# Finishing one token tile early at five seams of a two-block transformer kernel, and a query slot computed with tokens as rows

## The reference

```python
m = hybrid_mixer(h, ...)      # compressed, selected and window attention + short convolution, @ w_o
h = layer_norm(ALPHA * h + m, ln1_g[l], ln1_b[l])
f = swiglu(h, ...) if l % 2 == 0 else moe_swiglu(h, ...)
h = layer_norm(ALPHA * h + f, ln2_g[l], ln2_b[l])
```

## Time and profile before

| | |
|---|---|
| median of 3 runs | 1381.17 us |
| lowest, highest | 1379.94, 1381.62 us |
| the profiled execution, span from first to last instruction | 1380.5 us, mean granted clock 0.995 |
| TensorE matmul, share of the span | 98% |
| VectorE, ScalarE, GpSimd | 71%, 56%, 8% |
| loaded and stored | 306.33 MB, mean 222 GB/s |

### The profile page before, as it was taken

How to read it: one execution, slowest core, us unless ns; L and a number is a source line. 1 busy time by engine, 2 the same in 40 slices (tenths; PEclk the granted TensorE clock), 3 DMA queues, 4 the chain that set the end, 5 groups by cost and what they waited for, 6 DMA issues and landing times.

```text
span 1380.5 us, 21606 instructions
## 1 busy us (share of the span) xinstructions
PE 1350.9 (98%) x8554; PEld 1181.4 (86%) x8554; DVE 974.7 (71%) x1359; ACT 766.5 (56%) x932; POOL 104.7 (8%) x116
## 2 busy tenths in 40 slices
PE   7999999999999999999999999999999999999995
PEld 7998888878977888889999889888888888888884
DVE  6466476564867577766444466868898898898887
ACT  5565488334334338634433327743777677677673
POOL 1000031100002120002322010001000000000000
PEclk9999999999999999999999999999999999999998
DMA  7653443446543635435555545542989989999986
GB/s 282 228 184 123 151 144 134 156 166 226 188 147 145 236 133 202 165 123 182 204 183 180 197 155 192 199 173 100 367 320 348 335 328 348 338 329 357 334 330 244
DMA packets 44422, 306.33 MB, mean 222 GB/s; under 512 B 4960, under 2 KB 5216, under 8 KB 8752
## 3 DMA queue, kind: packets, MB, share of 16 engines
q1 hardware_dynamic: 42048, 296.22, 58.7%
q0 software_dynamic: 2288, 8.91, 1.9%
HBM read 304.07 MB, written 1.05 MB: 221 GB/s over the span
## 4 chain that ended last, share of the span: by engine, by line
PE 83%; DVE 7%; DMA 4%; ACT 3%; issue 2%; POOL 1%; SPq 0%; DVEq 0%; ACTq 0%
PE g_ps L604 18%; PE g_ps L606 18%; PE g_ps L605 17%; PE a_ps L604 6%; PE a_ps L606 6%; PE a_ps L605 6%; PE a_ps L609 5%; DMA raw<-w_dram 4%; PE a_ps L613 3%; PE o_ps L609 3%; DVE w_lo L1684 2%; ACT w_hi L1295 2%; POOL tiny L509 0%; DMA arena<-xT_dram 0%; DVE tiny L1727 0%
## 5 line engine op out<-in xcount | busy, mean ns | idle before, releaser
L1684 DVE TENSOR_TENSOR w_lo<-raw,w_hi 128x2048 fp32r<-128x2048 f32 x238 | 547.5, 2305 | 198.6 <-ACT w_hi L1295 196.3
L1295 ACT ACTIVATE w_hi<-raw 128x2048 fp32r<-128x2048 f32 x238 | 455.6, 1915 | 257.3 <-PE g_ps L606 92.6
L604 PE MATMUL g_ps<-x_hi,w_hi 128*128 128x256 f32 x880 | 252.1, 286 | 0.2 <-DVE w_lo L1684 0.2
L605 PE MATMUL g_ps<-x_lo,w_hi 128*128 128x256 f32 x880 | 249.3, 283 | 0.0
L606 PE MATMUL g_ps<-x_hi,w_lo 128*128 128x256 f32 x880 | 249.2, 283 | 0.0
L604 PE MATMUL g_ps<-w_hi,x_hi 128*128 128x512 f32 (+1 forms) x552 | 208.3, 377 | 3.0 <-DVE x_lo L1776 2.4
L606 PE MATMUL g_ps<-w_hi,x_lo 128*128 128x512 f32 (+1 forms) x552 | 203.5, 369 | 0.0
L605 PE MATMUL g_ps<-w_lo,x_hi 128*128 128x512 f32 (+1 forms) x552 | 203.2, 368 | 0.0
L604 PEld LDWEIGHTS g_ps<-x_hi,w_hi 128*128 128x128 f32 x880 | 169.1, 192 | 4.6 <-issue 4.1
L605 PEld LDWEIGHTS g_ps<-x_lo,w_hi 128*128 128x128 f32 x880 | 169.2, 192 | 0.0
L606 PEld LDWEIGHTS g_ps<-x_hi,w_lo 128*128 128x128 f32 x880 | 169.1, 192 | 0.0
(11 more groups left out here) (335 smaller groups left out, 1975.5 us busy)
## 6 DMA issues: line engine op xcount, KB each, us to landing
raw<-w_dram SPq DMA_DIRECT2D x277, 1024.0 KB, 4.9
arena<-rows_dram POOLq DMA_DIRECT2D x3, 1024.0 KB, 5.3
raw<-w_dram SPq DMA_DIRECT2D x4, 512.0 KB, 7.6
arena<-xT_dram SPq DMA_DIRECT2D x2, 512.0 KB, 5.3
x<-x_dram SPq DMA_DIRECT2D x2, 512.0 KB, 7.5
extra<-extra_dram POOLq DMA_DIRECT2D x1, 1024.0 KB, 5.0
extra<-rows_dram POOLq DMA_DIRECT2D x2, 512.0 KB, 3.9
y_spare<-rows_dram POOLq DMA_DIRECT2D x4, 256.0 KB, 4.3
```

What stands on the lines that cost most here:

```text
L604: pe.matmul(ps, lh, rh, start=start, stop=False, skip_group_check=True)
L605: pe.matmul(ps, lh, rl, start=False, stop=False, skip_group_check=True)
L1295: act.activation(w_hi[w_place(s)][:, :], raw[PLACE[s]][:, :], ACT.Copy).then_inc(hi_done, 1)
L1684: dve.tensor_tensor(w_lo[w_place(s)][:, :], raw[PLACE[s]][:, :], w_hi[w_place(s)][:, :].bitcast(F32), ALU.subtract).then_inc(lo_done, 1)
```

## The change

1. `out_tail` takes the place of `out_pair`. The last three slots (even layer), four (odd layer), three (feed-forward) run tile by tile. In the sparse layers the tail is slots 1, 2, 3 of four, of which slot 1's tile 0 is done earlier, among the attention's last steps. The transposes of tile 0 stand inside the tail, before the last slot's product for tile 1; in the feed-forward before its last column half.
2. `begin` no longer transposes tile 0, and `BUSY` is gone. Five fillers stay at seam 2, between `first` and `second`; seam 5 has 17 in `begin` in one place instead of 12 and 6. In all 61 fillers of this kind become 36.
3. In the sparse layers the first slot of q moves from s0+2 to s0+1 and is computed with tokens as rows, together with s0, for each tile. ScalarE copies the result to `q_rows`, TensorE transposes it with four transposes into the same bank after slot s0+2 (kc, vc), and ScalarE copies it to `sq`. The splits of the slots are reordered to match.
4. VectorE: the addition follows the new order of the banks; one split stands between the first and the second half of tile 1 at each seam (for slot 41, 73, 92, 125, 143), and at seam 2 the split of slot 72 comes after tile 0's norm. ScalarE at seam 2: the high parts of slots 72 and 73 before tile 1's first square, that of slot 74 before its second.

The diff, cut to its core:

```diff
-I_KC, I_Q, I_KS, ... = 1, (2, 4), 3, ...
+I_KC, I_Q, I_KS, ... = 2, (1, 4), 3, ...
+        q_rows = view(5056, (NT, S))
-        O_FULL = {1: 0, 2: 1, 3: 2, 4: 4, 5: 7}
+        O_FULL = {1: 0, 2: 2, 3: 4, 4: 6, 5: 9}
-        BUSY = {2: (8, 4, L_IN[0] + 2), 3: (0, 5, FFN_IN + 2), 4: (0, 12, L_IN[1] + 2), 5: (0, 12, None)}
+        EV_TAIL, OD_TAIL, FFN_TAIL = 3, 4, 3
...
+            def out_tail(i, s, order, first, second, ready):
+                end = len(order) - 1
+                for t, slots in enumerate((first, second)):
+                    for n in slots:
+                        pe.wait_ge(lo_done, s + n + 1)
+                        if t == 1 and n == end:
+                            for b in range(2):
+                                turn_rows_of(i, 0, b)
+                        mm = out_mm(s, order, n, t, ready(n) if t == 0 else None)
+                        if t == 1:
+                            mm.then_inc(used, 1)
+                        elif n == ends(order, order[n][1]):
+                            mm.then_inc(o_full, 1)
...
             def begin(i, first, second=None):
-                for b in range(2):
-                    turn_rows_of(i, 0, b)
-                if late and s is not None:
-                    keep_busy_before(late, s)
...
                 if second:
                     first(0, every)
+                    if i == 2:
+                        keep_busy_before(5, L_IN[0] + 2)
                     second(0, low)
...
                     first(0, every)
-                    keep_busy(6, 2, G_ALL)
+                    keep_busy(17, 2, G_ALL)
...
+                begin(2 + 2 * l, both, small_rows(2 + 2 * l, 1 + l))
+                rows_slot(s0 + I_KC)
+                pe.wait_ge(q_copied, l + 1)
+                for m in range(2):
+                    for t in range(NT):
+                        at = m * S + t * P
+                        tr = turned(g_ps[bank_of(s0 + I_Q[0])][:, at:at + P], q_rows[:, t, m * P:(m + 1) * P])
+                tr.then_inc(q_turned, 1)
                 fold_rows(1 + l)
...
# ScalarE, seam 2 and the sparse layers
+            for b in range(2):
+                squares_of(0, b)
+            for n in (4, 5):
+                ahead(OD_OUT + n)
+            squares_of(1, 0)
             hi_x(2, 0)
+            ahead(OD_OUT + 6)
             squares_of(1, 1)
-            ahead(OD_OUT + 6)
             hi_x(2, 1)
...
                 copy_slot(s0, ...)
+                act.wait_ge(used, s0 + I_Q[0] + 1)
+                act.activation(q_rows, g_ps[j] ..., ACT.Copy).then_inc(q_copied, 1)
+                ahead(s0 + I_Q[0])
                 act.wait_ge(narrow_full, 2 + l)
                 act.activation(rows24, a_ps[0][0:48, 0:S], ACT.Copy).then_inc(rows_copied, 1)
                 ahead(s0 + I_KC)
+                act.wait_ge(q_turned, l + 1)
+                act.activation(sq[:, 0:2, :], g_ps[j] ..., ACT.Copy).then_inc(g_free[j], 1)
...
# VectorE, seam 2
+                finish(2, 0)
+                dve.wait_ge(used, OD_OUT + 6)
+                plus(1, 0).then_inc(added, 1)
+                ahead(OD_OUT + 4)
+                low_half(2, 0, 0)
+                times_gain(1, 0)
+                summed(2, 1, 0)
+                low_half(2, 0, 1)
                 dve.wait_ge(used, OD_OUT + 8)
                 plus(1, 1).then_inc(added, 1)
-                low_part(2, 0)
+                ahead(OD_OUT + 5)
                 times_gain(1, 1)
...
# VectorE, seams 3 to 5
                 half(1, 0)
-                if i == 3:
-                    low_half(i, 0, 0)
+                if i != 5:
+                    low_part(i, 0)
+                ahead(mid)
                 half(1, 1)
```

More of the change, by code:

```diff
@@ L42 @@
 L_IN = (72, 124)
-I_KC, I_Q, I_KS, I_U, I_W1, I_C, I_B = 1, (2, 4), 3, (5, 7), (6, 8, 10, 11), (9, 12), (13, 14)
+I_KC, I_Q, I_KS, I_U, I_W1, I_C, I_B = 2, (1, 4), 3, (5, 7), (6, 8, 10, 11), (9, 12), (13, 14)
 L_WO = (87, 139)
@@ L954, in _ @@
             gates_and_out(11)
[L955 to L958, removed]
+            pe.wait_ge(y_split, 2 * OUT_EVEN[4][0] + 2)
+            out_slot(EV_OUT, OUT_EVEN, 4)
+            pe.wait_ge(y_split, 8)
+            tail = range(8 - EV_TAIL, 8)
+            out_tail(1, EV_OUT, OUT_EVEN, tail, tail, lambda n: None)
             begin(1, wide_part(1, OD_V, 0), wide_part(1, OD_V, 1))
@@ L1000, in _ @@
             pe.wait_ge(r_norm, RH)
-            for n in range(6):
+            for n in range(8 - OD_TAIL):
                 if n == 3:
@@ L1007, in _ @@
                     turn_outputs(6 + n)
-            out_pair(OD_OUT, OUT_ODD, False)
+            pe.wait_ge(r_lo, 8)
+            tail = range(8 - OD_TAIL, 8)
+            out_tail(2, OD_OUT, OUT_ODD, tail, tail, lambda n: None)
             def feed_forward(s0):
@@ L1032, in feed_forward @@
                 tiles = [(t, n) for t in range(NT) for n in range(2)]
-                for c in range(FT // 2 - 2):
+                tail = range(FT // 2 - FFN_TAIL, FT // 2)
+                for c in range(FT // 2 - FFN_TAIL):
                     pe.wait_ge(lo_done, s0 + FT + c + 1)
@@ L1812, in norm_after_even @@
                 dve.wait_ge(odd_gain_in, 16)
[L1813 to L1818 removed]
+                for b in range(2):
+                    dve.wait_ge(o_full, O_FULL[1] + b + 1)
+                    joined(1, 0, b, 1.0)
                 ready(1, 0)
                 finish(1, 0)
+                dve.wait_ge(used, EV_OUT + 6)
+                joined(1, 1, 0, 1.0)
+                low_part(1, 0)
+                ahead(EV_OUT + 5)
                 dve.wait_ge(used, EV_OUT + 8)
[L1822 to L1825 removed]
+                joined(1, 1, 1, 1.0)
                 ready(1, 1)
[L1827 removed]
                 finish(1, 1)
@@ L1870, in norm_after_odd, with scaled_norm @@
                     ahead(OD_OUT + n)
-            def scaled_norm(i, last, full):
+            def scaled_norm(i, mid, full):
                 dve.wait_ge(n_h, 4 * i)
@@ L1900, in scaled_norm @@
                     low_part(i, 1)
-                for s in () if i == 5 else (last, last + 1):
+                for s in () if i == 5 else (mid + 1, mid + 2):
                     ahead(s)
@@ L2236, in _ @@
                 s0 = L_IN[l]
-                ahead(s0)
+                for m in (0, I_Q[0]):
+                    ahead(s0 + m)
                 def blocks(s):
@@ L2260, in _ @@
                 dve.tensor_tensor(xs[:, :, 1, :], xc_all, xs[:, :, 0, :].bitcast(F32), ALU.subtract).then_inc(xc_split, 1)
-                for m in (I_Q[0], I_KS):
-                    ahead(s0 + m)
+                ahead(s0 + I_KS)
                 dve.wait_ge(gates_done, l + 1)
@@ L2346, in _ @@
                 i = 3 + 2 * l
-                for n in range(2):
-                    ahead(L_WO[l] + n)
-                scaled_norm(i, L_WO[l] + 2, [(o_full, O_FULL[i] + 1), (o_full, O_FULL[i] + 2),
+                ahead(L_WO[l])
+                scaled_norm(i, L_WO[l] + 1, [(o_full, O_FULL[i] + 1), (o_full, O_FULL[i] + 2),
                                              (used, L_WO[l] + 3), (used, L_WO[l] + 4)])
```

96 lines of the change are left out of this document (35 added, 61 removed).

## The result

The changed kernel takes **1384.06 us** (median of 16 runs, 1380.58 to 1389.52); the kernel before took 1380.82 in the same session (16 runs, 1379.37 to 1386.60). The ratio is **1.0023, with a 95% interval of 1.0014 to 1.0031**: slower by 3.2 us, where 1380.5 and "no change" was forecast. The time lies in the range, at its edge, and at the price of the clock rival (1384.6), which had 0.16.

The account below looks back on a forecast made before the run. TensorE was taken as the bound (busy 1350.9 of 1380.5 us, 61 matmuls being fillers). The terms 0.5 - 2.6 + 0.45 + 1.9 + 0.4 = 0.65 us came off, giving 1380.5 us; range 1376.5 to 1384.2.

Parts of the forecast that it names:

- seam 2: Odd layer's four tail slots into the first sparse layer: tile 1's transpose at 497.4, 2.45 us later than before.
- seam 5: Router seam after the second sparse layer: the 17 fillers decide, gain 0.4 us.
- the clock rival: Layer 0: new waits lower the clock, 1.56 us each, with the chain's loss at 3.5; 1384.6 us, chance 0.16.
- One more term has no sign that I can give: A fall of the granted clock, seen between 584 and 590, costs 1.56 us; it can go or come elsewhere.
- are no gain by themselves: All seams: removing 25 fillers (5.7 us) gains nothing alone, since tile 1's rows end each stretch.
- Seam 1: Even layer, three tail slots: tile 1's first half at 291.9, TensorE waits 0.8 us, gain 0.5.
- Seam 3: Sparse layer 0 into the feed-forward: rows at 627.0 instead of 627.46, wait 1.9 us, gain 0.45.
- Seam 4: Feed-forward, three tail slots: rows at 817.7 to 818.2, so no wait at tile 1's transposes (818.90 before).
- Layer 0: -2.6 forecast: First sparse layer: later loads and ScalarE's order delay the second scores by 2.2 to 3.5 us, 2.6 taken.
- TensorE sets the entry everywhere: Rival: loads and ScalarE's order have slack, layer 0 gains 1.0 instead of losing 2.6; 1376.9 us, chance 0.30.
- Layer 1: +1.9 forecast: Second sparse layer after the feed-forward: second scores at 853.7 instead of 855.63, gain 1.9 us (1.0 to 2.9).
- The rival that this gain doesn't come: Layer 1's chain is as long as layer 0's, so 1.9 shrinks to 0.5; 1381.9 us, chance 0.10.

Follow-up runs that it names:

- Experiment 1: The changed kernel run again with no edit, beside the kernel before: 1383.49 us, ratio 1.0020.
- experiment 4: The kernel before without the 41 fillers that BUSY places around tile 0's transposes: 1386.83 us, ratio 1.0030.
- Experiment 5: The changed kernel with 34 more fillers where TensorE waits: 1383.76 us, ratio 1.0021.
- Experiment 7: The changed kernel with ScalarE's square at seam 2 and its sparse-layer copies ahead of high parts that wait for loads: 1379.01 us, ratio 0.9995.
- 15: One more execution of the changed kernel with 34 more fillers in its waits: 1379.62 us.
- experiment 3: The kernel before with only the query slot moved and turned, tails and all 61 fillers as before: 1385.22 us, ratio 1.0032.
- 10: The kernel before with the query slot moved and turned and ScalarE's new sparse-layer order, old tails, all 61 fillers: 1383.09 us, ratio 1.0019.
- 13: The changed kernel with ScalarE's new orders and 15 more fillers, but query slot as before and 13 fillers replacing each moved tile: 1383.44 us, ratio 1.0018.

## Why the prediction was wrong

*What failed.* It is the step "One more term has no sign that I can give", with the rival "The new waits lower the clock" at 0.16. It entered the sum at nothing, and the term has a sign. I priced one fall about rightly (1.56; the new one at the router cost 1.0), but counted the falls from one profiled execution, in which the kernel before has one and none at the seams. Its executions differ, and what a change of waits moves is how often a fall comes, which a single profile can't show. Experiment 1 shows a mean clock lower by 0.0024 and puts 2 to 3 of the 3.0 us there, by the slope between clock and time; experiment 4 shows by an edit that this is what fillers hold back: without 41 of them the kernel before loses 0.0053 of mean clock and 6 us in the median (4.4 in the mean). Experiment 5 keeps this from being the whole account: fillers in the changed kernel's waits gave the clock back and 0.7 us. In the forecast's own words the 25 fillers that go "are no gain by themselves"; by experiment 4 taking them out is a loss. The rival's 1384.6 is nearly the time found, but half by luck: it is made of two falls, and of a loss of 3.5 us in layer 0 that didn't come. The argument against it, that 1.76 us of wait at seam 2 keeps its clock, does not carry: the same place with 2.2 us kept it in one execution of the changed kernel and lost it in the next. The bound that I named for the rival, query rows copied more than 1 us after slot 74 ends, was not reached in layer 0 (the transposes of the query rows wait for nothing there, those of layer 1 wait 0.73), and the falls came nevertheless.

*Seams.* Seam 1: 291.9 worked out, 291.92 found; wait 0.8 forecast, 0.54 found. Seam 2: ScalarE stands for the load as forecast, but until 489.21 and not 489.85 (tile 0's rows came half a microsecond sooner), and the transpose is at 496.74 instead of 497.4, its wait 2.21 for 2.3; TensorE's wait for the low part of the query slot 0.64 for 1.05. Seam 3: 626.64, forecast 627.0. Seam 4: 817.61 without a wait, as forecast at 817.7 to 818.2. Seam 5: 0.91 ahead of the kernel before, 0.34 of it since layer 1's second scores, where 0.4 was forecast. Here the working holds to half a microsecond.

*Layer 0: -2.6 forecast, -0.2 found.* Mis-sized, and not by the sum's own working: that gives 2.2 with a load of 4.95 us and 3.5 with 6.3, so 2.6 is nearer to the shorter of the two loads, and not "nearest to the longer" as it says. From seam 1's gain of 0.55 to the second scores' 0.33 the layer loses 0.2. The loads of the chain were 6.46 and 4.81 us, not 7.99 and 6.28, and the chain entered 0.65 sooner. The prediction's own measure (from the start of slot 68 to the second scores) is 69.4 us (463.41 to 532.81), where it was 69.2 and 71.8 was forecast. The rival "TensorE sets the entry everywhere" (0.30) did not come either: the layer gained no 1.0. Its 7.99 us load and GpSimd's row loads overlap in time but stand in two queues (q1 and q0), not in one.

*Layer 1: +1.9 forecast, -0.25 found* (0.82 ahead at seam 3, 0.57 at the second scores). The rival that this gain doesn't come, at 0.10, was right in that. What stands on the path is a coupling that I had not seen: slot 76 writes the bank in which the turned queries of slot 73 stand, so it (and slot 128 in layer 1) waits for ScalarE's copy of them (L1531), and that copy stands behind slot 130's high part (78's in layer 0), which stands for a load of 4.75 us. From that wait to the second scores it is 12.79 us in both layers (520.02 to 532.81, 842.27 to 855.06). I had followed slot 80's chain and taken ScalarE's order for a matter of that chain alone. Experiment 7 shows what ScalarE's order as a whole is worth: with its copies and square ahead of the high parts the second scores come 2.1 us sooner in layer 0 and 4.1 in layer 1, the fall taken out. No run moves the turned queries' copy alone, so its own share is not shown.

*The sum before the gather* came out at about 0.9 us where 0.65 was forecast (955.81 less one fall of 1.56 against 955.90 less 1.56 and 1.0), with its two large terms wrong by 2.4 and 2.2 against each other. That is luck, and a sum that is right in this way is no evidence for its terms.

*The base.* From an execution's span to its own time it is 1.8 us; the 0.7 that I carried over is the distance from one span to the median of other executions. The profiled execution of before had a fall and took 1382.3 us, 1.1 above the runs' median; mine was a comparison with an execution that already contained the thing whose sign I did not give.

*What stays open.* Whether 1.0 us is left at an equal clock, which hangs on the slope, and why experiment 5 got its clock back and not its time. The two profiled executions of the changed kernel have 425.9 and 425.5 us behind the gather, that of before 424.7, which is of the right size; but one kernel's executions differ by more than that (experiments 5 and 15). That the phase's length goes with TensorE's waits for split weights and for VectorE's small steps is shown; what sets those waits is not. The median weight load of the phase does not order the lengths: 6.5 us with 425.4 in experiment 3, 5.5 with 426.75 in experiment 5. Nor is it shown why the kernels of experiments 3, 10 and 13 stand 2 to 4 us above the kernel before at an equal clock (their four profiles have 425.4 to 429.1). It wasn't shown either which of the new waits costs which fall.

## What to carry to other kernels

Where a matmul engine's clock falls after slack, the mean granted clock over many executions is a result beside the time: count the filler work that a change takes out as a cost, unless real work fills the same place, and don't infer from one profile that a place is safe. When a change puts new copies on an engine that also does work waiting for loads, write down its queue in order: every copy that another engine, or a buffer's next writer, waits for goes ahead of the instruction that waits for a transfer. Here that order was worth about 4 us in the mean, 2.6 at an equal clock, more than the change itself had cost; and one copy of it 1.9 us without the change.

## What the runs showed that was not expected

The mean granted clock of whole executions differs by kernel in a way that single profiles hide: 0.9959 (112 executions of before), 0.9935 (28 of the changed kernel), 0.9906 (12 without 41 fillers), and about 1 us goes with each 0.001 (0.8 over all kernels, 0.9 and 1.2 in the first two). The falls don't keep to one place: in the changed kernel at 584 and 950 in one execution, at 496 and 834 in the next. In the kernel before, the gate rows' copy alone, moved ahead of a high part, took 1.9 us off. And the expert phase, the same instructions in all kernels, took 423.9 to 429.2 us, with no fall of the clock before its last matmul, in step with 1.8 to 5.8 us of small waits.
